# Low part of v on VectorE, a third place for u, and earlier reads around the value stage of a two-block model

## The reference, cut to what matters

```python
def chunk_fn(args):                       # hx: 128 tokens, ix: 128 experts a token, gx: their gates
    u = peer_u[ix]
    a = gelu(einsum('td,thkd->thk', hx, u))
    return einsum('thk,thkd->td', gx * a, peer_v[ix])
...
a = einsum('becd,edf->becf', xs, w_gate)  # second block: each of 16 experts takes its 64 best tokens
b = einsum('becd,edf->becf', xs, w_up)
y = einsum('becf,efd->becd', silu(a) * b, w_down)
```

## Time and profile before

| what | value |
|---|---|
| median of three runs | 3162.68 us (3160.28 to 3169.26) |
| profiled execution | 3163.25 us, of it span 3161.4 us |
| TensorE / VectorE / ScalarE / GpSimd busy | 85% / 43% / 26% / 31% of the span |
| moved by DMA | 869.99 MB, mean 275 GB/s |
| dots stage, TensorE's first to last matmul | 534.0 to 1200.0 us |
| value stage, the same | 1229.8 to 1775.0 us |
| MoE block, first matmul to the end | 2168.2 to 3161.4 us |

### The profile page before, as it was taken

One profiled execution on the slowest core, in us unless ns is written; L12 is line 12 of the kernel. 1 busy time (PEld: TensorE's weight loads), 2 busy tenths in 40 slices (PEclk: granted clock), 3 DMA queues, 4 the chain that ended last, 5 costly groups with the idle time before them and its releaser, 6 DMA issues. The chain is left out here.

```text
span 3161.4 us, 34451 instructions
## 1 busy us (share of the span) xinstructions
PE 2672.5 (85%) x12721; PEld 1850.8 (59%) x12721; DVE 1345.5 (43%) x2317; ACT 834.9 (26%) x1407; POOL 974.4 (31%) x485
## 2 busy tenths in 40 slices
PE   5986687999999995999999599964988788888886
PEld 2853577999999995877778476652323223222222
DVE  4346534995877765565665524444000000000001
ACT  2224221333666662333333222331000000000001
POOL 0030001666777775878878202000000000000000
PEclk8977788999999998999999799987999999999999
DMA  5333132445899998999999323117999999999996
GB/s 219 119 135 110 67 107 62 164 164 188 267 344 364 347 343 318 342 341 338 331 338 341 125 87 109 53 57 310 422 421 421 421 421 422 421 421 421 421 422 281
DMA packets 271859, 869.99 MB, mean 275 GB/s; under 512 B 28927, under 2 KB 122751, under 8 KB 219128
## 3 DMA queue, kind: packets, MB, share of 16 engines
q1 hardware_dynamic: 215136, 703.71, 58.7%
q0 software_dynamic: 38016, 138.43, 11.6%
q10 hardware_dynamic: 18584, 26.23, 2.2%
HBM read 812.69 MB, written 55.60 MB: 275 GB/s over the span
## 5 line engine op out<-in xcount | busy, mean ns | idle before, releaser
L562 PE MATMUL dots_dot_ps<-one_acts,dots_u_split 128*128 128x384 f32 x3072 | 556.5, 338 | 22.8 <-POOL dots_u_split L87 22.4
L689 PE MATMUL val_banks<-val_v,val_coef_split 128*128 128x512 f32 x2304 | 531.6, 391 | 43.5 <-DVE val_coef_split L87 43.0
L562 PEld LDWEIGHTS dots_dot_ps<-one_acts,dots_u_split 128*128 128x128 f32 x3072 | 534.0, 189 | 30.9 <-issue 22.6
L689 PEld LDWEIGHTS val_banks<-val_v,val_coef_split 128*128 128x128 f32 x2304 | 430.6, 188 | 144.3 <-issue 55.8
L934 PE MATMUL moe_up_ps<-all_raw_first,all_h_rows 128*64 128x512 f32 x1696 | 419.7, 605 | 69.3 <-DMA all_raw_first<-in_w_up 49.6
L87 POOL TENSOR_TENSOR dots_u_split<-dots_u_raw,dots_u_split 128x1024 fp32r<-128x1024 f32 x128 | 332.0, 2595 | 417.0 <-ACT dots_u_split L82 416.0
L934 PEld LDWEIGHTS moe_up_ps<-all_raw_first,all_h_rows 128*64 128x64 f32 x1696 | 138.8, 138 | 317.8 <-issue 316.6
L87 POOL TENSOR_TENSOR val_v<-val_v_raw,val_v 128x2048 fp32r<-128x2048 f32 x64 | 297.5, 4649 | 82.3 <-ACT val_v L82 82.2
L1053 DVE TENSOR_TENSOR all_x<-moe_y_ps,all_x 128x512 f32<-128x512 f32 x64 | 44.0, 691 | 560.6 <-PE moe_y_ps L900 560.5
L653 DVE SCALAR_TENSOR_TENSOR val_banks<-val_v_rows,one_slot_coef,val_banks 128x1024 f32<-128x1024 f32 x128 | 164.2, 1283 | 208.2 <-DMA val_v_rows<-in_peer_v,one_expert 208.0
L951 PE MATMUL moe_y_ps<-all_raw_first,moe_hid_t 128*64 128x512 f32 x848 | 206.8, 605 | 41.9 <-DMA all_raw_first<-in_w_down 22.8
(11 more groups left out here) (354 smaller groups left out, 3216.6 us busy)
## 6 DMA issues: line engine op xcount, KB each, us to landing
all_raw_first<-in_w_gate SPq DMA_DIRECT2D x106, 1024.0 KB, 27.3
all_raw_first<-in_w_up SPq DMA_DIRECT2D x106, 1024.0 KB, 27.6
all_raw_first<-in_w_down SPq DMA_DIRECT2D x106, 1024.0 KB, 27.3
dots_u_raw<-in_u_tiles SPq DMA_DIRECT2D x128, 512.0 KB, 4.4
val_v_raw<-in_peer_v SPq DMA_DIRECT2D x64, 1024.0 KB, 5.0
expert_dots<-dots_gelu ACTq DMA_DIRECT2D x128, 192.0 KB, 4.8
expert_weights<-pe_shared SPq DMA_DIRECT2D x48, 512.0 KB, 8.1
val_dot<-expert_dots SPq DMA_DIRECT2D x64, 384.0 KB
```

The costliest lines, as they stand in the source:

```text
L562: last = self.nc.tensor.matmul(self.banks[:, j, 0:DENSE], self.split[:, j, u_part, k], self.h_t[:, h_part, k, T - DENSE:T], start=(k == 0 ...
L689: last = nc.tensor.matmul(banks[:, 2 * (t + 1) + half, :], coef_split[:, b, c_part, a, t * P:(t + 1) * P], v[:, b, v_part, a, half * BANK: ...
```

## The change

Four things change.

1. `ExpertDots` gets a third place for u, made of two buffers that lie idle then: `h_row` for the raw tile, once VectorE has copied it (SP waits for `h_ready`), and the columns of the first 128 tokens of `h_t` for its parts. Banks and gelu stay at two (`OUT`). The loop has nine turns of six tiles in place of 28 of two. The sparse slots are spread over 67 of the 72 tiles.
2. The value stage's low part of v moves from GpSimd to VectorE; GpSimd only gathers. VectorE's turn is now: low part of v, low part of the coefficients, the next turn's coefficients, then two slots of the turn before. The gates of two turns come in one DMA, and SP asks for dots and gates before it waits for the rows' place; the SP loop is written out.
3. The value stage's buffers move into `shared` (class `ValueRows`), the memory of the stores' staging. Rows and dots of turns 0 and 1 are loaded at the end of the dots block, once the even spans are stored and before the last six parts of the odd span; the first gates are asked for behind all stores.
4. Eight MoE pieces are issued at the start of the MoE's block and not at the end of the router's.

The diff, cut (the helpers of `ExpertDots` change in the same way throughout, and so do the loops of the other engines):

```diff
--- before.py
+++ after.py
@@ -513,24 +513,28 @@
 class ExpertDots:
-    SLOTS = 2
-
-    def __init__(self, nc, s, A, h_t, dots_dram):
+
+
+    SLOTS, OUT = 3, 2
+
+    def __init__(self, nc, s, A, h_t, h_row, dots_dram):
         self.nc, self.A, self.h_t, self.dots_dram = nc, A, h_t, dots_dram
         n = self.SLOTS
-        self.raw = s.sb("u_raw", [P, n, KD, P])
-        self.split = s.sb("u_split", [P, n, 2, KD, P], F32R)
-        self.gelu = s.sb("gelu", [P, n, DENSE])
-        self.banks = s.ps("dot_ps", [P, n, BANK])
+        raw = s.sb("u_raw", [P, n - 1, KD, P])
+        split = s.sb("u_split", [P, n - 1, 2, KD, P], F32R)
+        self.raw = [raw[:, i] for i in range(n - 1)] + [h_row[:].rearrange("p (k e) -> p k e", k=KD)]
+        self.split = [split[:, i] for i in range(n - 1)] + [h_t[:, :, :, 0:P]]
...
@@ -538,58 +542,54 @@
         if name == "tensor":
             eng.sem_inc(self.dotted, self.SLOTS)
-    def load(self, sp, tile, turn, j):
+    def load(self, sp, tile, loop, q):
         sp.wait_ge(self.lo_ready, tile + 1)
-        sp.dma_start(self.raw[:, j], self.A["u_tiles"][bass.ds(tile, 1)].rearrange(
-            "a p k e -> p (a k) e")).then_inc(self.loaded[j], 16)
-
-    def split_scalar(self, act, tile, turn, j):
-        act.wait_ge(self.loaded[j], turn * 16 + 16)
+        sp.dma_start(self.raw[q % 3], self.A["u_tiles"][bass.ds(tile, 1)].rearrange(
+            "a p k e -> p (a k) e")).then_inc(self.loaded[q % 3], 16)
+
+    def split_scalar(self, act, tile, loop, q):
+        act.wait_ge(self.loaded[q % 3], loop * 32 + 16 * (q // 3) + 16)
         act.wait_ge(self.dotted, tile + 1)
-        split_hi(self.nc.scalar, self.split[:, j, 0], self.raw[:, j]).then_inc(self.hi_ready, 1)
-
-    def split_pool(self, pool, tile, turn, j):
+        split_hi(self.nc.scalar, self.split[q % 3][:, 0], self.raw[q % 3]).then_inc(self.hi_ready, 1)
+
+    def split_pool(self, pool, tile, loop, q):
         pool.wait_ge(self.hi_ready, tile + 1)
-        split_lo(self.nc.gpsimd, self.split[:, j, 1], self.raw[:, j],
-                 self.split[:, j, 0]).then_inc(self.lo_ready, 1)
-
-    def dot(self, pe, tile, turn, j):
+        split_lo(self.nc.gpsimd, self.split[q % 3][:, 1], self.raw[q % 3],
+                 self.split[q % 3][:, 0]).then_inc(self.lo_ready, 1)
...
+                      self.gelu[:, q % 2]).then_inc(self.stored[q % 2], 16)
+
+
+def peer_value_phase(nc, A, dots_dram, weight_dram, x, gate, expert, slot_coef, gathered, values):
     DT = DENSE // P
     with Scope(nc, "val") as s:
-        v_raw = s.sb("v_raw", [P, 2, 2, D])
+        v_raw, dot, weight, coef, part = values.raw, values.dot, values.weight, values.coef, values.part
         v = s.sb("v", [P, 2, 2, 2, D], F32R)
-        dot = s.sb("dot", [P, 2, 2, DENSE])
-        weight = s.sb("weight", [P, 2, SPANS, 2, SPAN])
-        coef = s.sb("coef", [P, 2, 2, DENSE])
         coef_split = s.sb("coef_split", [P, 2, 2, 2, DENSE], F32R)
-        part = s.sb("part", [P, 2, BANK])
         sparse = SparseTokens(nc, s, A["peer_v"], expert, "v", gathered)
         banks = s.ps("banks", [P, 8, BANK])
         sparse_sum = banks[:, 0:2, :].rearrange("p a n -> p (a n)")
...
@@ -602,18 +602,13 @@
         with nc.Block() as block:
             @block.sync
             def _(sp):
-                def load(turn, b, i):
-                    sp.wait_ge(v_lo, turn + 1)
-                    sp.dma_start(v_raw[:, b], A["peer_v"][bass.ds(turn * (2 * P), 2 * P), :].rearrange(
-                        "(a e) d -> e a d", e=P)).then_inc(v_loaded[b], 16)
-                    sp.wait_ge(coef_ready, turn * 2 + 2)
-                    sp.dma_start(dot[:, b], dots_dram[bass.ds(turn * 2, 2)].rearrange(
-                        "a e t -> e a t")).then_inc(c_loaded[b], 16)
-                    sp.dma_start(weight[:, b].rearrange("p s a t -> p s (a t)"),
-                                 weight_dram[:, :, bass.ds(turn * 2, 2), :].rearrange(
-                                     "s b a t -> b s (a t)")).then_inc(c_loaded[b], 16)
-
-                turns(sp, load)
+                for turn in range(2, n_turns):
+                    sp.wait_ge(coef_ready, 2 * (turn - 1))
+                    values.load_dots(sp, turn, dots_dram)
+                    if turn % 2 == 0:
+                        values.load_weights(sp, turn // 2, weight_dram)
+                    sp.wait_ge(v_lo, turn - 1)
+                    values.load_rows(sp, turn)
             @block.scalar
             def _(act):
...
                     act.wait_ge(summed, turn + 1)
                     split_hi(nc.scalar, v[:, b, 0], v_raw[:, b]).then_inc(v_hi, 1)
-                    act.wait_ge(coef_ready, turn * 2 + 6)
+                    act.wait_ge(coef_ready, turn * 2 + 2)
                     split_hi(nc.scalar, coef_split[:, b, 0], coef[:, b]).then_inc(coef_hi, 1)
                 turns(act, split)
...
                     sparse.gather(pool, c)
-                for turn in range(n_turns):
-                    b = turn % 2
-                    pool.wait_ge(v_hi, turn + 1)
-                    split_lo(nc.gpsimd, v[:, b, 1], v_raw[:, b], v[:, b, 0]).then_inc(v_lo, 1)
-                    for c in range(2 * turn + sparse.NR - 2, 2 * turn + sparse.NR):
-                        if sparse.NR <= c < P:
-                            sparse.gather(pool, c)
             @block.vector
             def _(dve):
-                dve.sem_inc(coef_ready, 4)
-                dve.sem_inc(coef_lo, 2)
...
                         in1=sparse_sum, op0=ALU.mult, op1=ALU.add).then_inc(sparse.used, 1)
-                for turn in range(n_turns):
-                    b = turn % 2
-                    dve.wait_ge(c_loaded[b], 32 * (turn // 2 + 1))
-                    dve.wait_ge(coef_lo, turn + 1)
+                def coefficients(turn):
+                    b, pair = turn % 2, turn // 2
+                    dve.wait_ge(dot_loaded[b], 16 * (turn // 2 + 1))
+                    dve.wait_ge(weight_loaded[pair % 2], 16 * (pair // 2 + 1))
+                    if turn >= 2:
+                        dve.wait_ge(coef_lo, turn - 1)
                     for a in range(2):
                         nc.vector.tensor_tensor(
                             coef[:, b, a].rearrange("p (s t) -> p s t", s=SPANS),
                             dot[:, b, a].rearrange("p (s t) -> p s t", s=SPANS),
-                            weight[:, b, :, a, :], ALU.mult).then_inc(coef_ready, 1)
-                    add_slot(2 * turn)
+                            weight[:, pair % 2, :, 2 * (turn % 2) + a, :], ALU.mult).then_inc(coef_ready, 1)
+
+                coefficients(0)
+                for turn in range(n_turns):
+                    b = turn % 2
+                    dve.wait_ge(v_hi, turn + 1)
+                    split_lo(nc.vector, v[:, b, 1], v_raw[:, b], v[:, b, 0]).then_inc(v_lo, 1)
                     dve.wait_ge(coef_hi, turn + 1)
                     split_lo(nc.vector, coef_split[:, b, 1], coef[:, b], coef_split[:, b, 0]).then_inc(coef_lo, 1)
-                    add_slot(2 * turn + 1)
+                    if turn + 1 < n_turns:
+                        coefficients(turn + 1)
+                    if turn >= 1:
+                        add_slot(2 * turn - 2)
+                        add_slot(2 * turn - 1)
+                add_slot(P - 2)
+                add_slot(P - 1)
                 step = Steps(dve, dve_step)
                 dve.wait_ge(sparse.used, P)
...
@@ -737,7 +735,7 @@
 class ExpertPieces:
-    FIRST, MORE = 14, 3
+    FIRST, MORE, EARLY = 14, 3, 6
     UNITS = 24
     SIZE = FF
@@ -834,7 +832,7 @@
         with nc.Block() as block:
             @block.sync
             def _(sp):
-                for n in range(pieces.FIRST, pieces.ring):
+                for n in range(pieces.EARLY, pieces.ring):
                     pieces.load(sp, n)
                 sp.dma_start(iota[:], rows(A["iota512"], P)).then_inc(iota_loaded, 16)
                 sp.dma_start(g_rows[:], rows(A["final_g_2"], P)).then_inc(g_loaded, 16)
...
@@ -1182,16 +1181,19 @@
         def slots_of(r):
-            return range(P * r // LEFT, P * (r + 1) // LEFT)
+            return range(min(P, P * r // (LEFT - 5)), min(P, P * (r + 1) // (LEFT - 5)))
         with nc.Block() as block:
             @block.sync
             def _(sp):
                 sp.dma_start(iota[:], rows(A["iota"], P)).then_inc(iota_loaded, 16)
-                with sp.Fori(0, CHOICE) as i:
-                    for j in range(2):
-                        dots.load(sp, i * 2 + j, i, j)
...
+                sp.wait_ge(h_ready, 1)
+                with sp.Fori(0, LOOPS) as i:
+                    for j in range(LOOP):
+                        dots.load(sp, i * LOOP + j, i, j)
+                for j in range(FIRST - LOOPS * LOOP):
+                    dots.load(sp, LOOPS * LOOP + j, LOOPS, j)
...
+                sp.wait_ge(stored[0], 16 * PARTS * (SPANS // 2))
+                for turn in range(2):
```

(33 more changed lines are left out.)

84 lines of the change are left out of this document (48 added, 36 removed).

## The result

The changed kernel took 3105.88 us (median of 4 runs, 3099.11 to 3107.42), the kernel before 3161.48 beside it: a ratio of 0.982, interval 0.980 to 0.984. The forecast was 3101, with a range of 3080 to 3132. The profiled execution took 3107.42 (span 3105.6), 55.8 less than that of before.

What follows compares the result with a forecast made beforehand. It took MoE weight traffic on full DMA engines as the chain of waits, with earlier stages running one after the other, so their savings come off the total. Terms summed to -61.9 us from 3163.25, giving 3101 us, range 3080 to 3132.

Steps and rivals of the forecast that it cites:

- Start: Before the dots stage: SP waits for DVE's copy of h_row before loading u, +0.6 us (0 to +1.2).
- Loop and third place: Dots stage's hardware loop: POOL may be a whole tile ahead, so stalls vanish, -11 us (0 to -11.6).
- First written-out tiles: Dots stage after the loop: one tile of lead covers PE's wait and slow matmuls behind gathers, -4.5 us (-2 to -4.6).
- Gate cycle: Written-out dots tiles with gate products: ACT splits earlier, gates come less late, 22.8 us per four tiles, -11 us (-18 to +3).
- rival (a): Queues are the bound: gate cycle gains nothing, value turn stays 8.35 us, hand-over loses 7; 3127 us, chance 0.12.
- Slots five tiles early: Last dots tiles: without POOL's gathers they take 22.6 us instead of 24.4, -2 us (0 to -2).
- first turns read early: Hand-over from dots to value stage: early rows and dots let PE start at +17, not +29.8, -13 us (-8 to -18).
- Value stage: Low part of v on DVE, gathers and requests earlier: waits go, 529 us stay of 545, -16 us (-8 to -21).
- MoE pieces: Router's end and MoE start: eight pieces issued in the next block, queues' pause closes, -5 us (0 to -5.2).
- (b): Hand-over: gates behind all stores and 2.9 MB put ahead eat the early reading; 3113 us, chance 0.11.
- (c): Dots loop: the larger body is fetched again at each of nine returns, +31 us; 3132 us, chance 0.05.
- (d): Value stage: DVE bounds it through stretched operations, 9.8 us a turn, +82 and not -16; 3199 us, chance 0.05.

Runs made afterwards that it cites:

- two_places: Two buffers of its own for u in place of three places, against the changed kernel: 3126.47 us, 21.3 more than the changed kernel run again.
- slots_72: Gathered slots of u spread over all 72 written-out tiles again instead of 67, against the changed kernel: 3106.84 us.
- late_reads: Rows, dots and gates of the first two turns asked for at the value block's start, behind all stores, against the changed kernel: 3106.76 us.
- the paired kernels: Changed kernel with DVE's order from before the change, low part of v on DVE (3104.91 us) or on POOL (3140.44 us).
- stores_spread: Changed kernel with first gates asked for ahead of the last six gate stores, these issued one a turn in the value block: 3097.81 us.

## Why the prediction was right, point by point

*The sum* was off by 4.9 us by the median, and by 6.1 in the profiled executions, of which 5.0 are the same code's longer time. The terms were less good than the sum: errors of opposite sign in it cancelled, and that is luck.

*Start:* as forecast in size (+0.6 forecast, +0.3 by PE's first matmul), but less than the scatter of that stretch, so it is not shown.

*Loop and third place:* right in mechanism and size (-11 forecast, -11.7 measured, +11.5 when undone). In all, the third place is worth 21.3 us.

*First written-out tiles:* -4.5 forecast, -3.3 measured, of which the third place gives 1.8 (two_places). The step "one tile of lead covers both" was too large: PE's first wait for POOL falls from 2.68 to 0.91 us and not to nothing, and two more, 1.6 and 1.1 us at the next tiles, which I had not counted, stay as they were.

*Gate cycle:* right in direction, too large by 3 to 5 us (-11 forecast, -7.9 and -5.9 in two profiles). The failed step is "if they never idle": I spread the stores evenly over the part, and where every tile has one, the queues set the pace. I took 22.8 us a cycle; it is 23.0 and 23.1. With fewer stored bytes (22.65) or fewer gathers a tile (slots_72, 350.5/15.5 = 22.6) it is there. So a part of rival (a) was true: the queues are the bound of this stretch, though not of the value stage, which ran at 8.16 us a turn.

*Slots five tiles early and first turns read early:* -15 together, -12.9 measured (-13.9 by PE's marks), but the causes were exchanged. "First turns read early" got -13 and is worth 0.5 (late_reads). The slots' end got -2: the last tiles gained 1.9, of which slots_72 undoes 1.2, and the hand-over gains 7.9 from it, for which the gate cycle pays 6 to 8, so it too brings about 2 us in all (1.1 to 3.1). Between slots_72's 25.7 us and the 29.8 of before lie 4.1 us that no run takes apart: late reads together with slots over 72 tiles were not tried. The queue's arithmetic (gates landed at +12.5 forecast, +13.5 measured) was right; wrong was to compare it with the old end of the block alone and not with the new end without early reads. In the kernel before, the slots did not hold the block alone. The timeline shows the last slot's result and SP's first read, 11 and 14 us after PE's last matmul (1199.98); the last store of gates, asked for at 1190.99, landed 20.3 us later, at 1211.3, and so ended with the slots.

```profile
1211.04 0.08 DVE L1392 DVE_READ_ACCUMULATOR2_ANT peer_slot_dot<- 128x1 f32 x1
...
1213.90 0.41 SPq L607 DMA_DIRECT2D val_v_raw<-in_peer_v  x1
```

*Value stage:* the mechanism was right, the size 4 us short: I left 3 us for branches and 2 for the cold start, and the stage took 64 x 8.16 = 522.2 and 2.5. The period in the earlier trace rows is 16.21+0.23 = 16.44 us, which makes 526 of 64 turns and not 524. The pause of 0.2 us in it was not a branch: PE's loop has the same form in the changed kernel, and its weight loads run there without a pause (45 us from 1425.0). Where I gave the credit to three edits, one has it: the engine of the low part (32 us between the paired kernels). The order brings nothing with the split on DVE (523.6 against 523.8 and 524.7), the requests nothing with it on POOL, and with POOL's split left in place the order costs 39 us more (594.4 against 555.5).

*MoE pieces:* -5 forecast, -4.2 measured, +3.7 to +6.1 when undone. The mechanism was right: the pause in the queues goes from 5.2 us to 2.3 in the changed kernel, and is gone where the transposes ahead of it run at the full clock.

*Rivals:* (b) was half true, since the reads put ahead of the stores gained almost nothing (0.5 us); (c) and (d) are ruled out by two_places and by DVE's turn of 6.9 us.

*Left open:* how the 21.3 us of the third place divide over loop, gates and hand-over when the queues are relieved was not tried. How the 32 us of the engine divide over late gathers and held products is open, as both go with the split on POOL. Nor was a way tried of narrowing the gate stores that keeps the result.

## What to carry to other kernels

A transfer put ahead of others on a full queue is paid for by those behind it: before crediting an early read, work out the end of the queue without it. When an engine's part seems stretched in its mean, look at median and maximum: here a product of 0.55 us had a maximum of 4.97, the length of another engine's instruction, and moving that instruction, not reordering around it, removed it. Give a block's last wait only what the next block's first step needs.

## What the runs showed of the hardware

DVE's two-input product and POOL's two-input split of v didn't run side by side: 0.55 us became 5.47 beside a split of 4.59, and with that in 59 of 64 turns DVE's product had a mean of 2.85 us. Something like it shows the other way too, untested by an edit: a gather's issue on POOL that began 0.08 us behind DVE's low part of v took 3.02 us, until both of DVE's low parts had ended, where it takes 0.94 (stores_spread). Others that began ahead of a low part kept their 0.94.

```profile
1184.40 2.29 DVE L87 TENSOR_TENSOR val_v<-pe_shared,val_v 128x2048 fp32r<-128x2048 f32 x1
...
1184.48 3.02 POOL L1127 DMA_INDIRECT val_v_rows<-in_peer_v,one_expert  x1 [11.58 <-issue]
```

The stretch from the program's start to the first gelu took 538 to 544 us in twelve profiles and 558.8 and 560.6 in two, with the same instructions. In those two the granted clock from 200 to 300 us was 0.60 in place of 0.69 to 0.73, and 0.84 in place of 0.91 to 0.94 from 400 to 500. The router's 32 transposes took 6.57 us in the changed kernel's two profiles (mean granted clock 0.55) and 3.69 in that of the kernel before (1.00): PE's rate at either of its two levels (1.2 and 2.4 GHz) decides some 3 us there, more than the smallest edits of this study.
